# A two-layer fp32 model kernel on one core: halved weight transfers for two experts, and another order of additions, low parts, router logits and mix waits

## The reference, cut to what matters

```
h = rms_norm(x, g);  parts = h @ w_in
x = x + (g_a * y_a + g_b * y_b + g_c * y_c) @ w_mix_o      # attention, gated unit, state space
h = rms_norm(x, g2)
group  = argmax(h @ router_group_w + b)                    # 4 groups of 8 experts
top2   = best two experts inside that group, softmax weights
y[t]   = sum over the two experts of w * (silu(h @ gate[e]) * (h @ up[e])) @ down[e]
x = x + y
```

## Time and profile before

| | |
|---|---|
| median of 3 runs | 1895.66 us (1894.4 to 1896.25) |
| the profiled execution | 1894.8 us, span 1893.1 us |
| granted TensorE clock, mean | 0.994 of full speed |
| TensorE busy | 1844.8 us (97%) |
| VectorE, ScalarE, GpSimd busy | 983.5, 489.2, 151.2 us |
| transfers | 482.13 MB, some 425 GB/s in the experts' stages |
| the experts' stages | 473 to 940 us and 1412 to 1877 us of the span |
| a pair of experts on TensorE | 29.6 us (downs start at 1608.66 and 1638.25); the last two pairs 26 us |
| gate and up of one expert at full clock | 6.9 us, 16 steps of two products, 0.43 us from step to step |

### The profile page before, as it was taken

One profiled execution on the slowest core, in us unless ns is written; L12 is line 12 of the kernel. 1 busy time (PEld: TensorE's weight loads), 2 busy tenths in 40 slices (PEclk: granted clock), 3 DMA queues, 4 the chain that ended last, 5 costly groups with the idle time before them and its releaser, 6 DMA issues. The chain is left out here.

```text
span 1893.1 us, 26671 instructions
## 1 busy us (share of the span) xinstructions
PE 1844.8 (97%) x10376; PEld 1153.3 (61%) x10377; DVE 983.5 (52%) x1925; ACT 489.2 (26%) x881; POOL 151.2 (8%) x241
## 2 busy tenths in 40 slices
PE   7999999999999999999889999999999999999996
PEld 3777777778445455454347877778774445454543
DVE  7755555767334343343477555557673344343444
ACT  4414444333111111111144234534331111111112
POOL 4600000050000000000055000000500000000000
PEclk9999999999999999999989999999999999999999
DMA  4222111344999999999732211114359999999995
GB/s 171 68 97 87 68 68 45 112 141 178 395 427 427 425 426 424 421 428 427 317 101 68 95 67 68 68 46 130 123 222 415 425 426 428 425 428 425 424 427 223
DMA packets 59952, 482.13 MB, mean 255 GB/s; under 512 B 9808, under 2 KB 22608, under 8 KB 30672
## 3 DMA queue, kind: packets, MB, share of 16 engines
q1 hardware_dynamic: 59856, 480.80, 62.6%
HBM read 476.59 MB, written 4.19 MB: 254 GB/s over the span
## 5 line engine op out<-in xcount | busy, mean ns | idle before, releaser
L1960 DVE TENSOR_TENSOR x_tokens<-x_tokens,ps 128x512 f32<-128x512 f32 x240 | 160.3, 686 | 216.6 <-PE ps L1097 215.4
L1121 PE MATMUL ps<-slabs,arena 128*64 128x512 f32 x512 | 226.7, 596 | 3.6 <-issue 3.6
L1112 PE MATMUL ps<-arena,branch 128*64 128x512 f32 x512 | 227.0, 595 | 0.5 <-ACT branch L1426 0.5
L1112 PE MATMUL ps<-slabs,branch 128*64 128x512 f32 x512 | 227.0, 595 | 0.0
L1122 PE MATMUL ps<-slabs,arena 128*64 128x512 f32 x512 | 226.7, 596 | 0.0
L1121 PE MATMUL ps<-arena 128*64 128x512 f32 x512 | 225.1, 592 | 0.0
L1122 PE MATMUL ps<-arena 128*64 128x512 f32 x512 | 225.0, 592 | 0.0
L835 PE MATMUL ps<-h_hi,w_parts 128*128 128x512 f32 x768 | 210.7, 408 | 1.5 <-DVE w_parts L1571 1.5
L1121 PEld LDWEIGHTS ps<-slabs,arena 128*64 128x64 f32 x512 | 70.3, 138 | 150.9 <-issue 150.9
L835 PEld LDWEIGHTS ps<-h_hi,w_parts 128*128 128x128 f32 x768 | 135.1, 189 | 38.8 <-issue 9.2
L1121 PEld LDWEIGHTS ps<-arena 128*64 128x64 f32 x512 | 70.0, 137 | 145.5 <-issue 145.1
(11 more groups left out here) (369 smaller groups left out, 3092.6 us busy)
## 6 DMA issues: line engine op xcount, KB each, us to landing
arena<-in_expert_w_gate SPq DMA_DIRECT2D x32, 2048.0 KB, 12.2
slabs<-in_expert_w_gate SPq DMA_DIRECT2D x32, 2048.0 KB, 15.2
slabs<-in_expert_w_up SPq DMA_DIRECT2D x32, 2048.0 KB, 19.6
arena<-in_expert_w_up SPq DMA_DIRECT2D x32, 2048.0 KB, 16.7
arena<-in_expert_w_down SPq DMA_DIRECT2D x32, 2048.0 KB, 9.6
slabs<-in_expert_w_down SPq DMA_DIRECT2D x32, 2048.0 KB, 14.0
slabs<-in_gate_w SPq DMA_DIRECT2D x24, 1024.0 KB, 4.8
slabs<-in_dense SPq DMA_DIRECT2D x22, 1024.0 KB, 5.9
```

The costliest lines, as they stand in the source:

```text
L1112: done = nc.tensor.matmul(ps[64 * b:64 * b + 64, BANK_Y[half], :], hidT[:, k, CAP * b:CAP * (b + 1)], w_down[b][:, k, half * 512:(half + 1 ...
L1121: nc.tensor.matmul(ps[0:64, BANK_GU[b], :], xk, low[:, k, :], start=(k == 0), stop=(k == ND - 1), tile_position=(0, 0))
L1960: v.tensor_tensor(xs, xs, ps[:, banks[n % len(banks)], :], ALU.add).then_inc(s["back_added"], 1)
```

## The change

It has six parts, in both layers.

1. **Third expert.** Gate and up of expert 2 are asked for in two halves of the chunks (columns 0 to 2047 and 2048 to 4095 of the place, 1024 KB each). The first halves are asked for when TensorE has used chunks 0 to 3 of expert 0 (new semaphore `gu_part`), the second halves at the time at which the whole was asked for. The loop on SP begins one step later.
2. **Last expert.** Gate and up of expert 31 are asked for at the same time as before, in two halves; the second halves count on a semaphore of their own (`last_half`), for which TensorE waits at chunk 4.
3. **Low parts.** The three `times` of `b_pow` are taken from ahead of `low_tokens(0)` and put behind `low_tokens(2)` (two of them) and behind the second `split_lo` (the third); `low_tokens(3)` comes ahead of that `split_lo`.
4. **Mix waits.** `mix` waits for a piece of `w_lo_pool` ahead of each of the four chunks j.
5. **Logits.** On TensorE `route_logits(2)` goes ahead of `mix_half(3, 1, 0)`, on VectorE `route(2)` ahead of `add_mix(3, 0)`.
6. **Additions.** In the last pair the slot's weight comes ahead of additions 4 to 7 and the selection between additions 5 and 6. The last additions go (0, 0), (1, 0), (0, 1), (1, 1), (2, 0), (2, 1), next_variance(0), (3, 0), (3, 1), as (tile, half); who waits for a tile waits for the count that this order gives.

```diff
--- before.py
+++ after.py
@@ -109,6 +109,7 @@

...
 QUAD = 4 * CAP
+GU_PARTS = 2

...
 def build(nc, io):
@@ -505,7 +506,7 @@
         w_in_sem = [[s["we0g"], s["we0u"], s["we0d"]], [s["we1g"], s["we1u"], s["we1d"]]]
...

-        shared = dict(xe_first="ov_hT_read", next_turned="ov_back", ...)
+        shared = dict(last_half="ov_added", gu_part="ov_hT", xe_first="ov_hT_read", next_turned="ov_back", ...)
           w_lo_pool="ov_selw", mix4_in="ov_selT")
...

@@ -601,13 +602,37 @@
         sp.dma_start(w_place[0][1], expert_rows(io["expert_w_up"], 0, ND)).then_inc(w_in_sem[0][1], 16)
...
         load_down(sp, 1, 1)
-        with sp.Fori(0, N_EXP // 2 - 1) as i:
+        for part in range(GU_PARTS):
+            if part < GU_PARTS - 1:
+                sp.wait_ge(s["gu_part"], part + 1)
+            else:
+                sp.wait_ge(s["gu_done"], 1)
+            cols = slice(part * SLAB // GU_PARTS, (part + 1) * SLAB // GU_PARTS)
+            for m, name in enumerate(("expert_w_gate", "expert_w_up")):
+                sp.dma_start(w_place[0][m][:, cols], expert_rows(io[name], 2, ND)[:, cols]).then_inc(w_in_sem[0][m], 16)
+        sp.wait_ge(s["gu_done"], 2)
+        load_gate_up(sp, 3, 1)
+        sp.wait_ge(s["down_done"], 2)
+        for b in range(2):
+            load_down(sp, 2 + b, b)
+        with sp.Fori(1, N_EXP // 2 - 2) as i:
             for b in range(2):
...
                 load_down(sp, 2 * i + 2 + b, b)
+        sp.wait_ge(s["gu_done"], N_EXP - 3)
+        load_gate_up(sp, N_EXP - 2, 0)
+        sp.wait_ge(s["gu_done"], N_EXP - 2)
+        for part in range(2):
+            cols = slice(part * SLAB // 2, (part + 1) * SLAB // 2)
+            landed = w_in_sem[1][0:2] if part == 0 else (s["last_half"], s["last_half"])
+            for m, name in enumerate(("expert_w_gate", "expert_w_up")):
+                sp.dma_start(w_place[1][m][:, cols], expert_rows(io[name], N_EXP - 1, ND)[:, cols]).then_inc(landed[m], 16)
+        sp.wait_ge(s["down_done"], N_EXP - 2)
+        for b in range(2):
+            load_down(sp, N_EXP - 2 + b, b)

...
         if last_layer:
@@ -622,7 +647,7 @@
             sp.dma_start(view(slab[0], SLAB), io["dense"][layer + 1, 0]).then_inc(slab_in[0], 16)
...
             for t in range(NT):
-                sp.wait_ge(s["back_added"], 4 * N_EXP - 8 + 2 * t + 2)
+                sp.wait_ge(s["back_added"], 4 * N_EXP - 8 + (3, 4, 6, 8)[t])
                 sp.dma_start(io["x_kept"][t * P:(t + 1) * P, :], x[:, t, :]).then_inc(x_saved, 16)
...
     @block.tensor
@@ -972,8 +997,9 @@
             k = MIX_SLABS[half][upper]
...
                 pe.wait_ge(s["w_hi_ready"], S_OUT + 3 + MIX_SPLIT.index(k))
-                pe.wait_ge(s["w_lo_pool"], LO_PIECES * (MIX_SPLIT.index(k) + 1))
             for j in range(4):
+                if t == 0:
+                    pe.wait_ge(s["w_lo_pool"], LO_PIECES * MIX_SPLIT.index(k) + j + 1)
                 if t == 0 and half == 0:
...
                 at = slice(t * P, (t + 1) * P)
@@ -1059,8 +1085,8 @@
         turn_h2(2)
...
         mix_half(3, 0, 1)
+        route_logits(2)
         mix_half(3, 1, 0)
-        route_logits(2)
         mix_half(3, 1, 1)
...
         gather_tile(0, 0)
@@ -1126,16 +1152,21 @@

...
             for b in range(2):
-                pe.wait_ge(w_in_sem[b][0], 16 * i + 16)
-                pe.wait_ge(w_in_sem[b][1], 16 * i + 16)
+                more = 0 if first or b == 1 else 16 * (GU_PARTS - 1)
+                pe.wait_ge(w_in_sem[b][0], 16 * i + 16 + more)
+                pe.wait_ge(w_in_sem[b][1], 16 * i + 16 + more)
                 if b == 1 and not first:
...
                 for k in range(ND):
+                    if last_quad and at == 3 and b == 1 and k == ND // 2:
+                        pe.wait_ge(s["last_half"], 32)
                     if b == 0 and q == 0 and k % 4 == 0:
...
                     done = gate_up(k, b, i, m, at)
+                    if first and b == 0 and k < ND - 1 and (k + 1) % (ND // GU_PARTS) == 0:
+                        done.then_inc(s["gu_part"], 1)
                 done.then_inc(s["gu_done"], 1)
...
             if not first:
@@ -1440,7 +1471,7 @@
         nc.scalar.activation(table_in, table_in, ACT.Sqrt).then_inc(s["table_in"], 1)
...
         def next_square(t):
-            act.wait_ge(s["back_added"], 4 * N_EXP - 8 + 2 * t + 2)
+            act.wait_ge(s["back_added"], 4 * N_EXP - 8 + (3, 4, 6, 8)[t])
             nc.scalar.activation(x_unit[:, t, :], x[:, t, :], ACT.Square, accum_out=sumsq[:, t:t + 1]).then_inc(s["next_sq"], 1)
...
         def next_root(t):
@@ -1544,12 +1575,6 @@
             link(v.tensor_tensor(to[:, 0].rearrange("p (a b) -> p a b", b=32), one[:, 0], two[:, 1], ALU.subtract))
...

-        for k in range(1, TB):
-            ins = times(b_pow[:, k - 1], bbar, k)
-            if k < TB - 1:
-                link(ins)
-        tell(ins, "bb_ready")
-
         def low_tokens(t):
...
             dve.wait_ge(s["proj_done"], J_SGU + t + 1)
@@ -1576,8 +1601,11 @@
         low_tokens(1)
...
         low_tokens(2)
+        link(times(b_pow[:, 0], bbar, 1))
+        link(times(b_pow[:, 1], bbar, 2))
+        low_tokens(3)
         split_lo(LO_PIECES)
-        low_tokens(3)
+        tell(times(b_pow[:, 2], bbar, 3), "bb_ready")
         dve.wait_ge(s["vsq_ready"], 1)
...
         dve.wait_ge(s["cparam_in"], 16)
@@ -1930,8 +1958,8 @@
         take_h2(2)
...
         placed(1)
+        route(2)
         add_mix(3, 0)
-        route(2)
         add_mix(3, 1)
...
         take_h2(3)
@@ -1983,8 +2011,9 @@
             if not first and not last_quad:
...
             hid_of(i, 1)
+            final = last_quad and at == 3
             if not first:
-                for n in range(0 if last_quad else 1, 8):
+                for n in range(0 if last_quad else 1, 4 if final else 8):
                     add_back(i, n, second, banks)
...
                 dve.wait_ge(s["x_gathered"], 2 * m + 3 + q)
@@ -1994,11 +2023,17 @@
                 dve.wait_ge(s["y_read"], 2 * i)
...
             v.tensor_reduce(w_slot, ps[:, BANK_SEL, :], AX, ALU.max).then_inc(s["slot_weight"], 1)
+            if final:
+                for n in range(4, 6):
+                    add_back(i, n, second, banks)
             if not first:
...
             dve.sem_inc(s["selT_read"], 1)
+            if final:
+                for n in range(6, 8):
+                    add_back(i, n, second, banks)
             for half in range(2):
...
                 cols = slice(half * 512, (half + 1) * 512)
@@ -2033,12 +2068,11 @@
                 pair(4 * j + at, 2 * j + at // 2, at, False, False, False)
...
             pair(12 + at, 7, at, False, False, True)
-        def last_add(t):
-            for half in range(2):
-                dve.wait_ge(s["back_done"], 4 * N_EXP - 8 + NT * half + t + 1)
-                dve.wait_ge(s["back_added"], 4 * N_EXP - 16 + 2 * t + half + 1)
-                xs = x[:, t, half * 512:(half + 1) * 512]
-                v.tensor_tensor(xs, xs, ps[:, BANK_X[t][half], :], ALU.add).then_inc(s["back_added"], 1)
+        def last_add(t, half):
+            dve.wait_ge(s["back_done"], 4 * N_EXP - 8 + NT * half + t + 1)
+            dve.wait_ge(s["back_added"], 4 * N_EXP - 16 + 2 * t + half + 1)
+            xs = x[:, t, half * 512:(half + 1) * 512]
+            v.tensor_tensor(xs, xs, ps[:, BANK_X[t][half], :], ALU.add).then_inc(s["back_added"], 1)

...
             dve.wait_ge(s["next_sq"], t + 1)
@@ -2051,14 +2085,18 @@

...
             dve.wait_ge(s["gfin_in"], 16)
-        last_add(0)
-        last_add(1)
+        last_add(0, 0)
+        last_add(1, 0)
+        last_add(0, 1)
+        last_add(1, 1)
+        last_add(2, 0)
+        last_add(2, 1)
         next_variance(0)
-        last_add(2)
+        last_add(3, 0)
+        last_add(3, 1)
         next_scale(0)
...
         next_variance(2)
-        last_add(3)
         next_scale(1)
...
```

More of the change, by code:

```diff
@@ L506, in build @@
         layer_sems = over_sems + [s[n] for n in names]
-        shared = dict(xe_first="ov_hT_read", next_turned="ov_back", nsa_parted="ov_silu", outp_free="ov_weights", m_hi_ready="ov_sel", m_lo_ready="ov_gathered", br_hi_ready="ov_xe", br_lo_ready="ov_gu",
+        shared = dict(last_half="ov_added", gu_part="ov_hT", xe_first="ov_hT_read", next_turned="ov_back", nsa_parted="ov_silu", outp_free="ov_weights", m_hi_ready="ov_sel", m_lo_ready="ov_gathered", br_hi_ready="ov_xe", br_lo_ready="ov_gu",
                       w_lo_pool="ov_selw", mix4_in="ov_selT")
```

## The result

| | before | after |
|---|---|---|
| median, first measurement | 1895.66 us | 1886.14 us (1884.91 to 1889.67, 5 runs) |
| ratio to before, 95% interval | | 0.995 [0.9933, 0.9967] |
| the profiled execution, span | 1894.8, 1893.1 | 1889.63, 1886.6 |
| outside the span | 1.7 | 3.0 |
| TensorE busy | 1844.8 | 1844.0 |

A forecast was written before the change was run, and what follows sets the result against it. TensorE, busy 1844.8 of 1893.1 us, sets the pace with the transfer queue just behind. Gains of 7.5 us in layer 0 and 5.6 in layer 1, together 13.1, give 1882.6 us on the median's scale; range 1879.9 to 1887.5.

The forecast's parts named there:

- Low parts: Ahead of the low tokens: TensorE's wait for the fourth goes whole; gain 1.2 us in layer 0, 1.5 in layer 1.
- mix waits: In the mix: chunks start at once instead of after GpSimd's fourth piece; gain 1.6 us in layer 0, 1.2 in layer 1.
- logits: Ahead of the rank: route(2) starts one half mix earlier and ends TensorE's wait; gain 0.87 us, in both layers 1.7.
- A rival said that the dense stages would take this back: Ahead of the attention and in the mix: TensorE's 2.7 + 2.8 us are lost at the next engine's wait; 1888.1 us, 9%.
- Third expert: Transfer queue behind down 1: earlier first halves of gate and up 2 close a hole of 2.3 us.
- the head start: Transfer queue: the lead from expert 2's halves lasts to down 31's landing; taken as 1.0 us, bounds 0 and 2.3.
- Last expert: At expert 31: wait and lower clock go, a new wait for down 31 in layer 0; gain 3.2 and 1.1 us.
- this form: Rival at the last downs: head start used up, TensorE waits for down 31; gains fall by 1.0 and 0.7 us; 20%.
- Additions: Last products and additions: earlier selection and denser order; gain 0.6 us ending layer 0, 0.9 ending layer 1.
- The slower rival: Four added transfers of a layer: each costs a fixed queue time, at most 2.8 us; slower by 6.4, 1902 us; 3%.

The follow-up runs named there:

- the cut one: The changed kernel with 12 products fewer in the skipped overflow block, so layer 1's first product stands at instruction 8665 instead of 8689; 1878.99 us, 0.9923.
- after again: The changed kernel as it stands, measured a second time beside before; 1887.31 us, 0.9954.
- the halves alone: Before with only the halved gate and up transfers of experts 2 and 31 (parts 1 and 2); 1894.6 us, 0.9994.
- the whole transfer for expert 2: The changed kernel with column halves of the last downs and the overflow block cut, but expert 2's gate and up asked for whole; 1878.17 us, 0.9913.
- the cut kernels: Four variants of the changed kernel without the products of three of eight gate and up chunks in the skipped overflow block; 1878.99, 1878.23, 1881.2 and 1878.17 us.
- before moved by 10 instructions: Before with 20 never-executed waits on TensorE in the overflow block, moving layer 1's first product from instruction 8679 to 8689; 1899.88 us, 1.0018.
- the rest alone: The changed kernel with before's whole transfers (parts 3 to 6 only); 1886.02 us, 0.9947; with the overflow block cut, 1881.2 us, 0.9931.
- the three kernels that were moved further: The changed kernel, and it with column halves of the last or all downs, with 12, 12 and 28 skipped waits; 1887.8, 1884.87 and 1905.65 us.
- Column halves of the last downs: The changed kernel with downs of experts 30 and 31 requested and awaited as column halves; 1884.06 us, 0.9937; with the overflow block cut, 1878.23 us, 0.9914.
- after moved by 6: The changed kernel with 12 waits in the skipped overflow block, moving layer 1's first product from instruction 8689 to 8695; 1887.8 us, 0.996.

## Why the prediction was right, and what it got wrong

**Low parts, mix waits, logits: right.** Forecast 3.7 and 3.6, measured 3.7 and 4.3 in after, and 4.1 and 4.4 in the cut one. The old order scatters in layer 0 (453.98 us in before, 454.96 and 456.20 in the two other kernels that have it), the new one hardly (449.4 to 450.3), so the 3.7 us there are rather the low end. In the mix of layer 0 the gain was 1.2 instead of 1.6: I had found VectorE's low part and the fourth piece ready together at 411.6, and the low part came last, 0.56 us late. A rival said that the dense stages would take this back; the table shows no sign of it.

**Third expert: the halves worked, the head start did not.** I wrote that a head start above 1.0 us is given back and took 1.0. All of it is given back by the end. Down 31 lands this long after the experts' first product: 455.5 and 454.3 us in before, 455.5 and 455.7 in after, 454.0 and 456.5 in after again, 454.4 and 454.3 with the halves alone, 454.8 and 454.9 without them. With or without halves it is 454 to 456.5. I had looked for the place where it is lost at 735.67 us; it goes earlier. Counted from the experts' first product, up 3 lands 2.1 us sooner than in before, and down 3 1.1 us, down 7 0.5 us; down 9 is 0.9 us later. The first loss is at the first downs behind the halves. They are asked for when TensorE is done with their places, at 496.21, with 2.7 us of transfers left in the queue, and down 2 lands 5.88 us after up 3 instead of 4.9. I had put the backlog that an issue needs at 2.8 us, so 2.7 should have cost 0.1 us, and cost 1.0. That the whole transfer for expert 2 ran as fast (1878.17 and 1878.23) agrees.

**Last expert: right in place, too high in size.** The wait moved to the downs, in both layers and not in one. The forecast gave this form 20%; in after it is what happened, with 2.2 and -1.0 us for the experts where I had 3.2 and 1.1. The term failed at the words "with the head start at 927.5": TensorE could not be early by more than down 31 was, and that lands when it did before. In the cut kernels both parts of transfers together were worth 1.5 to 2.2 us, of 4.3 forecast. In layer 1 there was next to nothing to win, because down 31 landed only 0.5 us before TensorE started on it. In layer 0 the cost of 4.3 us that I set out to remove, 2.48 us of wait and 1.8 by the clock, stood in the one profile that I read: before moved by 10 instructions has 1.06 us and no lower clock at the same place. Over four profiles with after's transfers the two stages together last 908.6 to 911.4 us, 910.5 in both profiles of the rest alone with whole transfers, 909.4 in before moved by 10, and 912.7 in before: the scatter of the queue, with single transfers 1 to 2 us late, is as large as the gain.

**Additions: right in layer 1, too low in layer 0.** The tail gave 1.0 us of 0.9. From the downs of the last pair to the last products it is 0.7 us in each layer. From there to the fourth tile of layer 1, the cut kernels take 37.2 to 39.3 us and before 40.3: 1.0 us or more beyond the 0.6 (the 37.2 is the profile at full clock). I had said that the turns start no earlier; they start 0.55 us later behind their products, but run through, where before's stood still for 0.6 us between the first tile and the others.

**Not in the sum: where the code lies.** This is the largest miss, 2.7 us of stall and 1.3 to 1.9 outside the span. I counted the added waits as three instructions a slab at no cost, which they are where they run. They lengthen TensorE's program in layer 0 by 10 instructions, six for the mix waits and four for the transfers. Between the layers every engine jumps over the overflow block. The page's list of queues shows how TensorE gets its code, 66 transfers of 16.4 KB, or 256 instructions of 64 bytes (packets, MB, share):

```profile
q8 instruction: 66, 1.08, 0.2%
```

In after, one of them runs in the stretch from 951.0 to 951.2 us (transfers of that stretch), when the other engines begin layer 1:

```profile
q8 instruction: 1, 0.02, 33.1%
```

VectorE's first instruction of layer 1 in the same profile:

```profile
951.00 2.48 DVE L1520 TENSOR_TENSOR hT<-ps,arena 128x512 f32<-128x512 f32 x4 [5.17 <-DVEq L2321]
```

TensorE starts at 953.74, 2.74 us after VectorE. In before the same transfer begins at 956.8, just behind the start of TensorE's first product, of which four stand ahead of 8687:

```profile
956.72 3.90 PE L683 MATMUL ps<-slabs,branch 128*128 128x512 f32 x5 [1.89 <-PEq L2283]
```

The transfers from 956.7 to 956.9 us:

```profile
q8 instruction: 1, 0.02, 37.5%
```

Those four, 0.8 us each at the lower clock, cover the fetch. With two ahead of it 0.84 us are left, with one 1.78, with none 2.7. In the three kernels that were moved further, to 8695 and 8711, the jump itself waits, 3.4 to 4.0 us, and once more at the end of the program, 3.5 to 3.7 us. The Trainium skill (Runtime: NRT & Kernel Launch, Instruction fetch mechanics) says that code comes in blocks of 16 KiB, 256 instructions, in order, and that a jump into a block that is not there yet waits for its transfer. The trace agrees, with 2.7 us for the wait. It is a rule against this change, and I did not weigh it.

The slower rival, a fixed time for each transfer, did not come: in a full queue the halves landed 2.47 us apart, half of the 4.9 of a whole one.

That the median lies inside the range is therefore in part luck: its 9.5 us hold two errors, 4 us or more lost to the code's place, against gains at the border and ahead of the experts above the forecast. Put back ahead of 8687, the same change is worth 15.0 us (0.9923). The interval runs from 12.1 to 17.2 us, so the 13.1 of the forecast are inside it.

**What beats both kernels.** Column halves of the last downs, with the code ahead of 8687: 1878.2 us, 0.9914; the cut change without them, 1879.0, can't be told from it by its time. The cut used here shortens a fallback that other inputs need; a loop in place of its unrolled products would do it properly, and was not tried. Nor was moving the jump itself into the next block.

## What to carry to other kernels

A transfer queue that is asked by the engine it feeds follows that engine: a head start shrinks at the first request that waits for the engine and is gone some requests later, and taking away a wait ahead of one transfer shows the next one's landing, so read the landing of the last transfer before counting the gain. Read it, and the wait that is to go, in more than one profile: here the same wait was 2.48 us in one and 1.06 in the next. Split a transfer along its long rows in memory, and along the order of use only where the queue has time to spare. And compare kernels that differ by a few microseconds at the same place of the program: move one by instructions that are never run, and look at the first wait behind each jump.

## What the runs showed that I had not expected

- Ten instructions that are never executed cost 4.0 us (1.0018 [1.0009, 1.0027]).
- The time outside the span is 3.0 to 3.6 us in every run of the kernels whose TensorE program has 17164 instructions (after, column halves of the last downs, before moved by 10), and 1.6 to 1.8 in the runs of all others (17144, 17152, 17156, 17176, 17208, 17116 and 17108). The three longest programs (17176 twice, 17208) pay inside the span instead, 3.5 to 3.7 us in TensorE's last jump where all others take 0.35, and a code transfer runs at that time (1882.1 us in after moved by 6). A code fetch would explain the time outside the span as well; the profile ends before it, so that is not shown.
- 1 MB in rows of 2 KB takes 2.7 us in a full queue, in rows of 8 KB 2.47.
- With some 12 us of transfers in rows of 2 KB outstanding, SP's issue of one took 3.9 us in place of 0.55; with 18.8 us in long rows it took 0.38. What limits it stays open.
